# Moving two activation tiles by 64 bytes and the tiles behind them by 256 bytes in SBUF: a two-model float32 block on one Trainium2 core

## What is computed

```
# first block, 2 layers
mix = dsa_mixer(h) if layer 0 else gla_mixer(h)          # sparse attention / gated linear attention
h = layer_norm(alpha * h + mix)
h = layer_norm(alpha * h + square(relu(h @ w_up)) @ w_down)   # w_up 1024 x 4096, w_down 4096 x 1024
# second block, 1 layer
h = rms_norm(x)
proj = h @ w_in                                          # q, k, v of two attentions, two convolutions
mixed = sum over 4 branches of sigmoid(h @ w_gate) * (branch @ w_branch)
x = x + rms_norm(mixed @ w_out)
x = x + rms_norm(cross_attention(rms_norm(x), mem) @ w_xo)
u = dwconv(rms_norm(x) @ w_up)                           # w_up 1024 x 5632
x = x + rms_norm((silu(u_g) * u_v) @ w_down)             # w_down 2816 x 1024
```

## The kernel before, in words

| tile | first byte | remainder by 256 |
|---|---|---|
| raw0, whi0, wlo0 (and all 12 ring buffers) | 16512, 49280, 82048 | 128 |
| h, z | 114816, 123008 | 128 |
| xh, xl | 131200, 139392 | 128 |
| consts | 147584 | 128 |
| fh, fl | 170176, 186560 | 192 |
| bhi, blo | 213952, 218048 | 192 |
| gh, gl | 170176, 192704 | 192 |

## Time and profile before

### The profile page before, as it was taken

One profiled execution on the slowest core, in us unless ns is written; L12 is line 12 of the kernel. 1 busy time (PEld: TensorE's weight loads), 2 busy tenths in 40 slices (PEclk: granted clock), 3 DMA queues, 4 the chain that ended last, 5 costly groups with the idle time before them and its releaser, 6 DMA issues.

```text
span 1332.1 us, 25095 instructions
## 1 busy us (share of the span) xinstructions
PE 1283.2 (96%) x10634; PEld 1245.3 (93%) x10634; DVE 888.7 (67%) x1374; ACT 642.5 (48%) x834; POOL 46.3 (3%) x40
## 2 busy tenths in 40 slices
PE   9989999999987999999999999999999999999997
PEld 8868999999987999999999999899998989999997
DVE  6875764565568567646565459899766655899843
ACT  5464453443453335435435444554454454777631
POOL 0561000000000000000000000000000000000000
PEclk9999999999998999999999999999999999999999
DMA  9222255455331134554533543334454241454430
GB/s 358 97 107 95 98 190 202 175 189 189 130 127 64 64 127 156 192 190 163 204 111 128 189 163 129 144 138 168 149 187 168 94 154 64 158 185 173 177 128 32
DMA packets 28505, 198.41 MB, mean 149 GB/s; under 512 B 3440, under 2 KB 3952, under 8 KB 4736
## 3 DMA queue, kind: packets, MB, share of 16 engines
q1 hardware_dynamic: 27792, 195.83, 40.5%
q10 hardware_dynamic: 624, 1.31, 0.3%
HBM read 196.08 MB, written 1.05 MB: 148 GB/s over the span
## 4 chain that ended last, share of the span: by engine, by line
PE 79%; DVE 11%; ACT 4%; issue 2%; DMA 2%; POOL 2%; DVEq 0%; ACTq 0%
PE lin L462 23%; PE lin L464 23%; PE lin L463 23%; DVE wlo L1471 3%; PE lin L544 3%; PE att L537 2%; DVE conv L1950 2%; DMA raw<-units_dram 2%; ACT whi L1029 1%; PE lin L567 1%; POOL pr L447 1%; DVE qk L1812 1%; DVE z L1562 0%; POOL lg L447 0%; DVE h L1568 0%
## 5 line engine op out<-in xcount | busy, mean ns | idle before, releaser
L462 PE MATMUL lin<-xh,whi 128*128 128x256 f32 x1936 | 555.7, 287 | 3.9 <-DVE xl L1525 2.1
L1471 DVE TENSOR_TENSOR wlo<-raw,whi 128x2048 fp32r<-128x2048 f32 x179 | 409.6, 2291 | 212.3 <-ACT whi L1029 211.6
L463 PE MATMUL lin<-xl,whi 128*128 128x256 f32 x1936 | 549.8, 284 | 0.0
L464 PE MATMUL lin<-xh,wlo 128*128 128x256 f32 x1936 | 549.5, 284 | 0.0
L1029 ACT ACTIVATE whi<-raw 128x2048 fp32r<-128x2048 f32 x183 | 348.6, 1907 | 180.6 <-PE lin L464 167.3
L462 PEld LDWEIGHTS lin<-xh,whi 128*128 128x128 f32 x1936 | 373.5, 193 | 8.7 <-issue 5.5
L463 PEld LDWEIGHTS lin<-xl,whi 128*128 128x128 f32 x1936 | 373.6, 193 | 0.6 <-issue 0.5
L464 PEld LDWEIGHTS lin<-xh,wlo 128*128 128x128 f32 x1936 | 373.4, 193 | 0.0
L462 PE MATMUL lin<-fh,whi 128*128 128x256 f32 x512 | 143.4, 280 | 0.0
L463 PE MATMUL lin<-fl,whi 128*128 128x256 f32 x512 | 142.8, 279 | 0.0
L464 PE MATMUL lin<-fh,wlo 128*128 128x256 f32 x512 | 142.8, 279 | 0.0
(11 more groups left out here) (336 smaller groups left out, 1600.9 us busy)
## 6 DMA issues: line engine op xcount, KB each, us to landing
raw<-units_dram SPq DMA_DIRECT2D x183, 1024.0 KB, 4.8
h<-x_dram SPq DMA_DIRECT2D x1, 1024.0 KB, 6.9
memT<-mem_dram ACTq DMA_DIRECT2D x1, 1024.0 KB, 4.8
out_dram<-h SPq DMA_DIRECT2D x4, 256.0 KB, 2.0
consts<-consts_dram SPq DMA_DIRECT2D x1, 864.0 KB, 15.6
narrow_a<-narrow_a_dram SPq DMA_DIRECT2D x1, 544.0 KB, 8.7
vec<-vectors_dram SPq DMA_DIRECT2D x1, 245.5 KB, 17.8
posi<-pos_dram SPq DMA_DIRECT2D x1, 128.0 KB, 8.6
```

The lines of the kernel that those rows point to most:

```text
L462: mm(out, w[0], a[0], start=first, stop=False)
L463: mm(out, w[0], a[1], start=False, stop=False)
L464: return mm(out, w[1], a[0], start=False, stop=last)
L1471: v.tensor_tensor(wlo[u % RING][:], raw[u % RING][:], whi[u % RING][:].bitcast(f32), ALU.subtract).then_inc(lo_ready, 1)
```

## The change

Two tensors that nothing reads or writes are placed around `xh` and `xl`, 64 and 192 bytes per partition:

```diff
         h = sbuf("h", [P, DB, S])
         z = sbuf("z", [P, DB, S])
+        sbuf("ahead_of_x", [P, 16])
         xh = sbuf("xh", [P, DB, S], f32r)
         xl = sbuf("xl", [P, DB, S], f32r)
+        sbuf("behind_x", [P, 48])
         consts = sbuf("consts", [P, NC])
```

## The result

The changed kernel takes **1319.15 us** (median of 4 runs, 1314.49 to 1324.25), the kernel before 1335.65 us in the runs beside it (4 runs, 1333.67 to 1338.17). The ratio is 0.9885, 95% interval 0.986 to 0.991, so it is 15.4 us faster, between 12.0 and 18.7. The forecast was 1326.3 us and a gain of 11.3: the direction and the mechanism came out, the size is larger than forecast. The runs of the changed kernel spread over 10 us where those of before spread over 4.5; that belongs to the explanation.

What follows compares the result with a forecast made beforehand. The prediction took TensorE's matmul steps to bound the kernel. Shorter steps of 13.4 us less 2.1 us hidden gave 11.3 us, from the median 1337.6 to 1326.3 us, range 1320 to 1332.

Steps and rivals of the forecast that it cites:

- TensorE bounds the kernel, and a shorter step comes through: Whole program: TensorE works 96% of the span, VectorE and ScalarE wait for it; 11.3 us gain expected.
- the sum that the prediction took off: Stretches where other work or waiting hides faster matmuls, such as gated attention and convolution: 2.1 us lost from the gain.
- The pace of a step belongs to the tile's offset, not to the code: Matmul steps in `unit_wide`: 120.0 ns with `xh`, 117.7 with `bhi`, by the tile's remainder by 256 relative to the weights.
- The rule that placement changes nothing: All matmul steps: the skill's two independent read ports, read as leaving the time at 1337.6 us; cited under the region rival.
- The lower bound of 112 ns, loading 128 float32 columns: Large products: the weight load alone takes about 112 ns, so a step can't be shorter.
- 117.7 ns for streamed tiles, from three tiles at that offset: Steps streaming `xh` or `xl`, 5808 of them: from 120.0 to 117.7 ns, as `fh`, `bhi` and `gh` have.
- 5842 x 2.3 ns = 13.4 us: All steps on `xh` and `xl` lasting 119 to 121 ns, each shortened by 2.3 ns: 13.4 us before hidden parts.
- `unit_tok` at 117.7, the weakest term: The 528 steps that load `xh` or `xl` and stream weights: 117.7 ns instead of 120.0, worth 1.2 us.
- Rival 1: Only the streamed operand's own remainder counts, so `unit_tok` stays at 120: gain 10.3 us, 1327.3 us; chance 0.27.
- Rival 2, region or other causes: The memory region of `xh` and `xl`, or another cause untouched by the shift, sets the pace: 1337.6 us; chance 0.11.
- Rival 3, a bad reverse offset: In `unit_tok`, load 64 bytes ahead of stream may collide: slower, 1379 us at the 219 ns upper bound; chance 0.02.
- Later tiles, `fh`, `bhi`, `gh`, writes by other engines: Later tiles keep their remainder by 256, and other engines' accesses to `xh` and `xl` are few: nothing gained or lost.

Runs made afterwards that it cites:

- e12: The changed kernel measured once more, unaltered, in a second comparison with the kernel before: 1321.97 us, ratio 0.9909.
- e5: Against the kernel before, `xh` and `xl` moved by 32 bytes instead of 64, later tiles as in the changed kernel: 1320.08 us, ratio 0.9893.
- e6: Against the kernel before, `xh` and `xl` moved by 192 bytes, the rest of 256 bytes behind them: 1316.99 us, ratio 0.9864.
- e1: Against the kernel before, whole SBUF layout moved up 64 bytes, ring buffers included, so stream and load keep offset 0: 1331.86 us, ratio 1.0007.
- e4: Separate kernel with only the matmul triples, eight tiles at offsets 0 to 224 bytes, streamed then loaded; gives the map of paces, 113.3 to 120.0 ns a step.
- e10: Against the kernel before, `xh` and `xl` placed ahead of the ring buffers, all activation tiles 64 bytes below the weights' remainder: 1306.13 us, ratio 0.9797.
- e2: Against the kernel before, all 256 bytes of padding ahead of `xh`, none behind `xl`; later tiles as in the changed kernel: 1334.78 us, ratio 1.001.

## Why the prediction was right, and where it fell short

- *TensorE bounds the kernel, and a shorter step comes through.* Right. Of 16.7 us of shorter steps at least 12 came through; e12, whose clock is like that of before (0.988 and 0.989), has 21.0 us of shorter steps and 18.9 us of time, so 2.1 us hidden, the sum that the prediction took off. That the two agree so closely is in part luck: counted the same way e5 has 21.1 us of shorter steps and 13.6 of time, e6 23.5 and 12.1, of which the lower clock of their profiled executions (0.986 and 0.984, some 6 and 12 us more at 1.2 GHz) explains up to 3 and 6. That leaves over 4 and over 5 us hidden. What hides them in e5 and e6 isn't shown.
- *The pace of a step belongs to the tile's offset, not to the code.* Right, and now shown: e1 puts `xh` on the changed kernel's own bytes and has 120.0 ns, since the weights moved along; e4 has the same paces without any other engine. The trace of before could only argue it. That stream and load get in each other's way in the memory is still an inference from these paces.
- *The rule that placement changes nothing.* The Trainium skill ("SBUF — State Buffer", "Who interferes with whom") states that TensorE has two independent read ports, one for the stream and one for LDWEIGHTS, and never waits on anyone. By the prediction's reading of it, no placement changes a step and the time stays at 1337.6 us. The measurement decides against that reading: in e4, where no other engine works, the step is 113.3 to 120.0 ns by the offset alone.
- *The lower bound of 112 ns, loading 128 float32 columns.* The number stands, its reason doesn't. The prediction held that 128 float32 columns stream in half of 106.7 ns, so that 112 ns could only be the load. But rows of before with only 8 columns to load take (715.0 - 711.7) / 15 = 220 ns a matmul for 256 float32 columns, by the start times 216, so 128 of them need some 108 ns and the earlier trace rows alone can't tell stream from load. What tells them is a row with 64 streamed columns by 128 loaded ones: 32 of them lie between 455.51 us and the start of the next instruction at 459.03, so 110 ns each, by the start times 111 or 112 but for the first two.

```profile
L885 PE MATMUL lin<-z,narrow_f x16: 379/379/382, 711.7 to 715.0; 128*8 128x256 f32 x16
...
455.51 3.68 PE L544 MATMUL lin<-consts,z 128*128 128x64 f32 x32
```

- *117.7 ns for streamed tiles, from three tiles at that offset.* Right for nine steps in ten, and **the term that was mis-sized**. "5842 x 2.3 ns = 13.4 us" should have been 16.5. At this offset there is a second state of 113.3 ns, which the 2448 steps of before at the same offset never showed. In the first trace 730 steps were in it, 730 x 4.4 = 3.2 us, in the second 1637. The lower bound of 112 ns covered it; I used it as a bound and gave no chance to anything between. The count of 5842 steps at 119 to 121 ns should have been 5942, which is 0.2 us.
- *`unit_tok` at 117.7, the weakest term.* It was 116.2 on the mean (120.0 before), part 117.7 and part 113.3. Rival 1 gave it 120 and is refuted, by this and by e1. Its price of 1.0 us was too high by the prediction's own working, since 192 of the 528 steps lie in the stretch from 368 to 427 us, which it counted as hidden; 336 x 2.3 ns = 0.8 us.
- *Rival 2, region or other causes*: ruled out by e1 and e10. *Rival 3, a bad reverse offset*: no offset of the map costs more than 120.0, so offset 0 was among the worst already.
- *Later tiles, `fh`, `bhi`, `gh`, writes by other engines*: nothing, as forecast (e2). In the 46 steps of `bhi` from 871 us on, at an unchanged offset, the 113 ns state showed up by itself.
- *The range.* The median of 1319.15 us lies 0.85 below its low end of 1320. Against the 1337.58 us that the forecast started from, the ratio gives 0.9885 x 1337.58 = 1322.2, inside it; the runs of before had meanwhile a median 2 us lower. The low end was the full gain at 117.7 ns against the fastest run. With the 113 ns state in it, it should have reached below 1314.49, the fastest of the four runs.

## What to carry to other kernels

When TensorE runs long rows of matmuls with a weight load each, read the start-to-start time per operand tile, and where the same function has different paces on different tiles, compare the tiles' byte offsets to the weights' modulo 256. Here 64 bytes of padding gave 1.2% (0.9% in the second comparison) and a layout with all streamed tiles 64 bytes below the weights' remainder 2.0%, with no instruction changed. But 8 bytes can lie between the best pace of the map and the worst, so measure the offsets instead of assuming that any is good. When a layout changes for other reasons, a gain or loss of 1% can come from this alone.

## What the runs showed that I had not expected

- Two states at one offset. At an offset of 64 bytes either way a row of steps in the full kernel settles within a few steps at 117.8 or at 113.3 ns. In the traces of the changed kernel, e6, e10 and e12 it keeps it to its next pause or to the next change of tiles or roles, where it can change without a pause (e6, at 189 us, from `xh` to `fh`); the longest is 1118 steps in e12, on `xh` and `xl` and then `gh` and `gl`. The state of 113.3 ns is commoner where the stream is 64 bytes below the load: in the changed kernel 36% of the steps of `unit_tok`, which are so, against 10% of those that stream `xh` and `xl`, and 45% against 25% in e12. Over three steps the paces 113.3, 117.8 and 120.0 are 340.0, 353.3 and 360.0 ns, so 13.3 and 20.0 ns above the lowest.
- At offset 0 most rows begin unevenly behind a pause and settle at 120.0 within some ten steps (e4, first block of `xa`: 117, 118, 117, 118, 120, 120, 117, 118, and 120 from then on). The slow pace is also one that a row falls into.
- Offsets of 184 and 200 bytes are as bad as 0 and 96 (120.0 ns), with 192 between them at 113.3 or 117.8.
